# State space layer: where the discretisation stands in the first MLP, and in what pieces the scans stand among the attention's rows

## Chip, core and metric

The kernel runs on one core of one Trainium2 chip. The metric is the device time of one execution in microseconds (us); the median of three runs is quoted. The profile is one further execution with its own time. TensorE is written PE, VectorE DVE, ScalarE ACT, GpSimd POOL, and SyncE SP.

## What is computed

Six layers run one after the other on a sequence of 512 tokens with 1024 features (batch 1, fp32). The change touches two of them: the first gated MLP (stage `ffn0`) and the layer after it (stage `ssm`), in which a diagonal state space model and a latent attention read the same normed input and are joined by one output product.

```python
    dt = jnp.exp(log_dt.astype(f32))[:, None]
    mag = jnp.exp(lr * dt)
    ab_re = mag * jnp.cos(li * dt)
    ab_im = mag * jnp.sin(li * dt)
...
    _, _, x_re, x_im = lax.associative_scan(combine, (aa_re, aa_im, bu_re, bu_im), axis=1)
    y = (jnp.einsum('bsgp,ghp->bsgh', x_re, c_re.astype(f32))
         - jnp.einsum('bsgp,ghp->bsgh', x_im, c_im.astype(f32))
         + d_skip.astype(f32)[None, None] * ug)
    y = y.reshape(b, s, SSM_CHANNELS).astype(u.dtype)
    z = jax.nn.gelu(y)
    return z * jax.nn.sigmoid(z @ w_glu + b_glu)
...
        sc = jnp.einsum('bqhd,bkhd->bhqk', qb, k, preferred_element_type=f32) * scale
        p = jax.nn.softmax(jnp.where(chunk_causal_mask(i, s), sc, -jnp.inf), axis=-1)
        return jnp.einsum('bhqk,bkhd->bqhd', p.astype(v.dtype), v)
...
def swiglu(h, w_gate, w_up, w_down):
    return (jax.nn.silu(h @ w_gate) * (h @ w_up)) @ w_down
```

Here `lr` and `li` are `a_re` and `a_im`; the attention has 6 heads and 4 blocks of 128 queries. The discretisation (`dt`, `mag`, the cosines and sines, `f`) depends on parameters alone, not on the layer's input.

## The kernel before

All engines run the same six stages, and each engine's program is written by walking one list of steps, `STEPS[stage]`. A step such as `("s1", i)` makes each engine issue its own instructions for that name, if it has any, so the list fixes the order of every engine's queue. Engines wait for each other through semaphores alone. `merge(a, b)` interleaves lists in proportion to their lengths: the longer one list is in steps, the more evenly it lies in the other, and where a step falls depends on the lengths of both.

**Products.** A weight tile is 128x128. It is split into a high and a low part, and `("w", g, k)` issues three matmuls of 512 columns on PE (lines 570 to 572). Weights come in slots of eight tiles: SP loads, ACT rounds the high part (line 624), POOL subtracts to get the low part (line 2586), PE waits for the slot. There are three slots for the split weights, and ACT rounds two slots ahead.

**Stage ffn0.** 22 gates in three thirds. `fg` and `fu` are gate and up products of eight k each in two banks each; `e1`, `e2`, `e3` evict, multiply by the sigmoid, and split the result for the down products. `pend` holds those steps of one gate, and they are merged into the products of the next. `closing` is the last third's down product in eight groups of seven: three banks (4, 5, 6) in turn, which the DVE addition on line 697 frees; then comes the sum of squares for the norm (lines 610, 612), which the next stage needs. Before the change the eight steps `("ds", 0)` to `("ds", 7)`, the discretisation, are merged into all but the last 24 steps of this closing. They are chains of small DVE operations, each waiting for the one before it (lines 2133 to 2232), and on ACT `ds 0` (two Exp) and `ds 4` (four Sin with a table load ahead and one behind, lines 2388 to 2392). The last of them, `cim`, is awaited by the first softmax row of the next stage.

**Stage ssm.** The attention runs in three pairs of heads, 24 units (a head's block of 128 queries, with 512, 384, 256 or 128 keys), taken two by two. `r1` puts both units' scores into banks 2 and 3 (PE, lines 2078 to 2083); `r2` takes the row maximum (DVE, line 2290) and then the exponential (ACT, line 2454); `r3` is reciprocal and diagonal (DVE); `r4` transposes and scales the weights (PE, line 2092, copied out by ACT, line 2462); `v1`, `v2` are the values' product. The next `r1` waits until ACT has read both banks, that is for the second unit's exponential, and that waits for its maximum in DVE's queue. Besides the rows there stand the next heads' projections and the first half of the output product (`p`), evicted by ACT (line 2494).

The scan has eight parts `i`. `s1`: two small matmuls on PE (lines 2113, 2114), then four DVE products with the angles' cosine and sine (2311 to 2314). `s2`: two additions (2320, 2322) and two scans over 512 tokens (2324, 2326). `s3`: six operations that turn the result back (2332 to 2341). `s4`: eight matmuls for two parts (2125, 2127). `z1` to `z4` are the GELU, a chain through DVE and ACT, and then the product `zg`, which waits for `z_low` (line 2369). POOL computes the angles (`an`, lines 2532 to 2542); `an 5` to `an 7` wait for line 2337 of an earlier part.

Of the kernel before, what the change touches and what calls it, by code (L numbers as in the profile page):

```python
# [243 lines left out]

def steps_ffn(*besides):

    out = []
    for third, (a, b) in enumerate(THIRDS):
        pend = []
        for f in range(a, b):  # L250
            g, u = ("fg", f), ("fu", f)
            if f == 0:
                mul = opening(g, u, ("fg", 1))
            elif f == 1:
                mul = merge(group(u, 8), pend)
            else:
                mul = merge(group(g, 8) + group(u, 8), pend)
            out += mul
            pend = [("e1", f), ("e2", f), ("e3", f)]
        out += pend  # L260
        if third < 2:
            out += groups([("d", third, d) for d in range(KT)], b - a, "de")
    last = closing(THIRDS[2][1] - THIRDS[2][0])
    return out + merge(last[:-24], besides) + last[-24:] if besides else out + last

# [16 lines left out]
def steps_ssm():  # L282
# [20 lines left out]
    for i in range(0, 8, 2):  # L303
        scan += [("s1", i), ("s2", i), ("s1", i + 1), ("s3", i), ("s2", i + 1), ("s3", i + 1)]
        scan += [("an", n) for n in {0: (5,), 2: (6,), 4: (7,)}.get(i, ())]
        scan += [("s4", i)]
        if i % 4 == 2:
# [4 lines left out]


STEPS = {"even": steps_even(), "odd": steps_odd(), "diff": steps_diff(), "ffn0": steps_ffn(*[("ds", n) for n in range(8)]),
         "ssm": steps_ssm(), "ffn1": steps_ffn()}


# [163 lines left out]
def program(nc, io):  # L481
    with ExitStack() as ctx:
# [1751 lines left out]
        def dve_ssm(e):  # L2234
            s = S["ssm"]
            pe, dve, act, pool = s.pe, s.dve, s.act, s.pool
            for step in STEPS["ssm"]:
# [65 lines left out]
                elif kind == "s1":  # L2303
# [7 lines left out]
                    e.tensor_tensor(vre, ps[6][:], cosT, MUL).then_inc(dve.sem, dve.up("s_a", i))  # L2311
                    e.tensor_tensor(vim, ps[7][:], cosT, MUL).then_inc(dve.sem, dve.up("s_b", i))
                    e.tensor_tensor(w5, ps[7][:], sinT, MUL).then_inc(dve.sem, dve.up("s_c", i))
                    e.tensor_tensor(w6, ps[6][:], sinT, MUL).then_inc(dve.sem, dve.up("s_d", i))
                elif kind == "s2":
                    i = step[1]
                    vre, vim, w5, w6 = lane_of(i)
                    mg = mag[:, i:i + 1].to_broadcast([128, T])
                    e.wait_ge(dve.sem, dve["s_c", i])
                    e.tensor_tensor(vre, vre, w5, ADD).then_inc(dve.sem, dve.up("s_re", i))  # L2320
                    e.wait_ge(dve.sem, dve["s_d", i])
                    e.tensor_tensor(vim, vim, w6, SUB).then_inc(dve.sem, dve.up("s_im", i))
                    e.wait_ge(dve.sem, dve["s_re", i])
                    e.tensor_tensor_scan(w5, mg, vre, 0.0, MUL, ADD).then_inc(dve.sem, dve.up("scan_re", i))
                    e.wait_ge(dve.sem, dve["s_im", i])
                    e.tensor_tensor_scan(w6, mg, vim, 0.0, MUL, ADD).then_inc(dve.sem, dve.up("scan_im", i))
                elif kind == "s3":
# [5 lines left out]
                    e.wait_ge(dve.sem, dve["scan_im", i])  # L2333
                    e.tensor_tensor(vim, w6, cosT, MUL).then_inc(dve.sem, dve.up("s_f", i))
                    e.wait_ge(dve.sem, dve["s_f", i])
                    e.tensor_tensor(w6, w6, sinT, MUL).then_inc(dve.sem, dve.up("s_g", i))
                    e.tensor_tensor(w5, w5, sinT, MUL).then_inc(dve.sem, dve.up("s_h", i))
                    e.wait_ge(dve.sem, dve["s_g", i])
                    e.tensor_tensor(vre, vre, w6, SUB).then_inc(dve.sem, dve.up("s_i", i))
# [40 lines left out]
        def act_discretise(e, n, dve, act):  # L2380
# [4 lines left out]
            elif n == 4:  # L2385
# [5 lines left out]
                e.activation(tabs, a6, ACT.Sin, scale=6.283185).then_inc(act.sem, act.up("tabs"))  # L2391
                e.preload_act_table_set(EXP_LN)

# [365 lines left out]
```

## Time and profile before

| what | value |
|---|---|
| median of 3 runs | 2060.03 us (2060.03 to 2063.84) |
| the profiled execution | 2062.9 us, its span 2061.1 us |
| PE busy | 1815.9 us, 88% of the span |
| DVE, ACT, POOL busy | 951.9, 740.2, 925.8 us |
| chain that ended last | PE 71%, DVE 17%, ACT 7% |
| mean granted TensorE clock | 0.934 of 2.4 GHz |

The span is the time from the first to the last instruction; what lies around it is 1.8 us. PE carries most of the chain that ends last, so a microsecond in which PE waits is in general a microsecond of the kernel.

### The profile page before, as it was taken

The page shows a single profiled execution, that of the slowest core. Times are in us where ns is not written, and L with a number is a line of the kernel's source. Part 1 is how long each engine was busy: PE and PEld are TensorE (multiplying, and loading weights), DVE is VectorE, ACT ScalarE, POOL GpSimd, SP SyncE. Part 2 cuts the span into 40 slices and gives each one's busy share as a digit, 9 for nine tenths or more (in the row PEclk, how much of TensorE's full clock was granted, in tenths as well). Part 3 has the DMA queues.
Part 4 walks back from the last instruction along what each step waited for, and adds up shares of the span by engine and source line. Part 5 has one row for each costly group of instructions (what it writes and reads, how often), then busy time and mean ns, then how long its engine had stood idle before and what let it go on. Part 6 is the DMA issues. An engine that isn't in the chain of part 4 may idle for free.

```text
span 2061.1 us, 20065 instructions
## 1 busy us (share of the span) xinstructions
PE 1815.9 (88%) x7492; PEld 1363.4 (66%) x7492; DVE 951.9 (46%) x1451; ACT 740.2 (36%) x1207; POOL 925.8 (45%) x1100
## 2 busy tenths in 40 slices
PE   5999889888878898878999999988777889999996
PEld 4776456666756576455788888755454568888885
DVE  1033333677562599754430323564755554123244
ACT  4253454445344422364332322342232342322232
POOL 3433113464753354113565656468222246565563
PEclk9999999998988899988999999998778899999998
DMA  4211102212111222012233323211000122333231
GB/s 167 92 62 52 41 21 73 70 62 72 50 33 34 69 80 74 21 31 72 73 95 99 102 93 102 82 62 51 11 11 21 31 64 90 103 92 102 93 94 70
DMA packets 39553, 139.90 MB, mean 68 GB/s; under 512 B 4512, under 2 KB 4640, under 8 KB 39328
## 3 DMA queue, kind: packets, MB, share of 16 engines
q1 hardware_dynamic: 39456, 138.61, 21.1%
q8 instruction: 60, 0.98, 0.2%
q14 instruction: 37, 0.30, 0.0%
HBM read 136.50 MB, written 2.10 MB: 67 GB/s over the span
## 4 chain that ended last, share of the span: by engine, by line
PE 71%; DVE 17%; ACT 7%; issue 2%; POOL 1%; DMA 0%; SPq 0%; DVEq 0%; ACTq 0%; POOLq 0%
PE ps L570 18%; PE ps L571 17%; PE ps L572 17%; DVE ps L1689 3%; PE ps L599 2%; PE ps L583 1%; PE ps L2101 1%; PE ps L585 1%; PE ps L584 1%; PE ps L818 1%; PE ps L820 1%; POOL wl L2586 1%; PE ps L2078 1%; ACT wh L624 1%; PE ps L811 1%
## 5 line engine op out<-in xcount | busy, mean ns | idle before, releaser
L2586 POOL TENSOR_TENSOR wl<-raw,wh 128x256 fp32r<-128x256 f32 x988 | 801.7, 843 | 998.7 <-ACT wh L624 990.8
L570 PE MATMUL ps<-hh,wh 128*128 128x512 f32 x1204 | 518.5, 431 | 70.2 <-DVE hl L687 45.8
L571 PE MATMUL ps<-hl,wh 128*128 128x512 f32 x1204 | 479.5, 398 | 0.0
L572 PE MATMUL ps<-hh,wl 128*128 128x512 f32 x1204 | 478.9, 398 | 0.0
L624 ACT ACTIVATE wh<-raw 128x1024 fp32r<-128x1024 f32 x247 | 261.1, 1058 | 554.8 <-PE ps L572 507.5
L570 PEld LDWEIGHTS ps<-hh,wh 128*128 128x128 f32 x1204 | 233.2, 194 | 149.1 <-DVE hl L687 51.8
L570 PE MATMUL ps<-mh,wh 128*128 128x512 f32 x632 | 267.6, 423 | 46.1 <-DVE ml L1324 6.5
L571 PEld LDWEIGHTS ps<-hl,wh 128*128 128x128 f32 x1204 | 232.7, 193 | 61.4 <-issue 17.7
L572 PEld LDWEIGHTS ps<-hh,wl 128*128 128x128 f32 x1204 | 232.1, 193 | 50.8
L571 PE MATMUL ps<-ml,wh 128*128 128x512 f32 x632 | 254.2, 402 | 0.0
L572 PE MATMUL ps<-mh,wl 128*128 128x512 f32 x632 | 253.9, 402 | 0.0
L570 PEld LDWEIGHTS ps<-mh,wh 128*128 128x128 f32 x632 | 123.2, 195 | 95.8 <-issue 12.2
L572 PEld LDWEIGHTS ps<-mh,wl 128*128 128x128 f32 x632 | 123.3, 195 | 27.3
L571 PEld LDWEIGHTS ps<-ml,wh 128*128 128x128 f32 x632 | 124.3, 197 | 23.7 <-issue 2.0
L1899 DVE TENSOR_TENSOR ml<-arena,mh 128x512 fp32r<-128x512 f32 x44 | 34.7, 789 | 119.5 <-ACT mh L1930 119.5
L1888 DVE TENSOR_TENSOR arena<-ps,nrm 128x512 f32<-128x512 f32 x44 | 30.4, 691 | 127.7 <-PE ps L572 127.7
L1689 DVE SCALAR_TENSOR_TENSOR ps<-arena,vec,ps 128x512 f32<-128x512 f32 x116 | 87.4, 753 | 2.9
L1886 DVE TENSOR_TENSOR arena<-ps,nrm 128x512 f32<-128x512 f32 x44 | 29.9, 680 | 100.0 <-PE ps L572 100.0
L919 DVE SCALAR_TENSOR_TENSOR arena<-ps,nrm 128x128 f32<-128x128 f32 (+3 forms) x32 | 15.6, 488 | 109.5 <-ACT nrm L1005 109.5
L687 DVE SCALAR_TENSOR_TENSOR hl<-x,vec,hh 128x512 fp32r<-128x512 f32 x48 | 40.3, 839 | 53.1 <-ACT hh L639 53.1
L583 PE MATMUL ps<-wh,hh 128*128 128x512 f32 x128 | 52.1, 407 | 9.3 <-DVE arena L1160 9.2
L655 ACT ACTIVATE nrm<-arena 128x512 f32<-128x512 f32 x48 | 30.1, 627 | 77.2 <-DVE arena L697 77.1
(464 smaller groups left out, 2297.2 us busy)
## 6 DMA issues: line engine op xcount, KB each, us to landing
raw<-in_w SPq DMA_DIRECT2D x247, 512.0 KB, 3.5
x<-in_x SPq DMA_DIRECT2D x8, 256.0 KB, 6.9
out<-x SPq DMA_DIRECT2D x8, 256.0 KB, 2.0
arena<-in_rope SPq DMA_DIRECT2D x3, 512.0 KB, 4.8
arena<-in_dec SPq DMA_DIRECT2D x1, 1024.0 KB, 11.6
mats<-in_mats SPq DMA_DIRECT2D x1, 576.0 KB, 7.8
arena<-in_lw SPq DMA_DIRECT2D x1, 512.0 KB, 3.8
arena<-in_levels SPq DMA_DIRECT2D x1, 448.0 KB, 4.5
```

The lines of the kernel that those rows point to most:

```text
L570: e.matmul(ps[b][:], a, xh, start=first, stop=False)
L571: e.matmul(ps[b][:], a, xl, start=False, stop=False)
L572: e.matmul(ps[b][:], l, xh, start=False, stop=final).then_inc(pe.sem, pe.up(*step))
L583: e.matmul(ps[i][:], hh[:, k, cut(i)], a, start=(k == 0), stop=False)
L599: e.matmul(ps[7][:], M("ones"), sqr[k % 2], start=(k == 0), stop=(k == KT - 1)).then_inc(pe.sem, pe.up("sq", k))
L624: e.activation(wh[:, n % NHL, :], raw[:, n % NRAW, :], ACT.Copy).then_inc(rounded.sem, rounded.up(n))
L655: e.activation(sqr[d % 2], y[:, d, :], ACT.Square).then_inc(act.sem, act.up("oe", d))
L687: e.scalar_tensor_tensor(out=hl[:, k, :], in0=x[:, k, :], scalar=V(PRE[stage], k), in1=hh[:, k, :].bitcast(F32), op0=MUL, op1=SUB).then_in ...
L1689: e.scalar_tensor_tensor(out=yb[:, j, :] if q == 30 else conv_in[j], in0=du[:, j, q:q + T], scalar=V("dww", 4 * q + j), in1=conv_in[j], op ...
L1888: e.tensor_tensor(f_up[f % 2], ps[bank(stage, ("fu", f))][:], rb_pre, MUL).then_inc(dve.sem, dve.up("e", ("fu", f)))
L1899: e.tensor_tensor(ml[:, i, :], f_up[f % 2], mh[:, i, :].bitcast(F32), SUB).then_inc(dve.sem, dve.up("mixed", f))
L2586: e.tensor_tensor(wl[:, n % NHL, cut(i, 2)], raw[:, n % NRAW, cut(i, 2)], wh[:, n % NHL, cut(i, 2)].bitcast(F32), SUB).then_inc(split.sem, ...
```

## The change

The eight discretisation steps leave the closing of `ffn0` and stand among its gates: `ds 0` behind the opening, `ds 1`, `2`, `3` behind the gates 1, 2, 3, `ds 4` behind gate 5, `ds 5` behind gate 7 (it is then followed by the first third's down products), and `ds 6` and `7` behind the gates 8 and 9. Behind `ds 4` ACT loads the sigmoid table in place of the Exp and Ln table. In the stage `ssm` no operation is added or removed, but `s1`, `s2`, `s3` are cut into eight steps (`s1`, `s1b`, `s2`, `s2b`, `s2c`, `s3`, `s3b`, `s3c`), and the list `scan` grows from 41 steps to 81, so that `merge(mul, scan)` puts the pieces, and also `s4`, `an` and `z1` to `z4`, at other places.

```diff
-def steps_ffn(*besides):
+def steps_ffn(**besides):
...
-            pend = [("e1", f), ("e2", f), ("e3", f)]
+            pend = [("e1", f), ("e2", f), ("e3", f)] + besides.get(f"f{f}", [])
+            if f == 0:
+                out += besides.get("first", [])
...
-    last = closing(THIRDS[2][1] - THIRDS[2][0])
-    return out + merge(last[:-24], besides) + last[-24:] if besides else out + last
+    return out + closing(THIRDS[2][1] - THIRDS[2][0])
...
     for i in range(0, 8, 2):
-        scan += [("s1", i), ("s2", i), ("s1", i + 1), ("s3", i), ("s2", i + 1), ("s3", i + 1)]
+        scan += [("s1", i), ("s1b", i), ("s2", i), ("s2b", i), ("s1", i + 1), ("s1b", i + 1), ("s2c", i), ("s3", i), ("s3b", i)]
+        scan += [("s3c", i), ("s2", i + 1), ("s2b", i + 1), ("s2c", i + 1), ("s3", i + 1), ("s3b", i + 1), ("s3c", i + 1)]
         scan += [("an", n) for n in {0: (5,), 2: (6,), 4: (7,)}.get(i, ())]
         scan += [("s4", i)]
...
-STEPS = {"even": steps_even(), "odd": steps_odd(), "diff": steps_diff(), "ffn0": steps_ffn(*[("ds", n) for n in range(8)]),
+STEPS = {"even": steps_even(), "odd": steps_odd(), "diff": steps_diff(), "ffn0": steps_ffn(first=[("ds", 0)], f1=[("ds", 1)], f2=[("ds", 2)], f3=[("ds", 3)], f5=[("ds", 4)], f7=[("ds", 5)],
+                                                                         f8=[("ds", 6)], f9=[("ds", 7)]),
...
                     e.tensor_tensor(vre, ps[6][:], cosT, MUL).then_inc(dve.sem, dve.up("s_a", i))
                     e.tensor_tensor(vim, ps[7][:], cosT, MUL).then_inc(dve.sem, dve.up("s_b", i))
+                elif kind == "s1b":
...
                     e.tensor_tensor(vim, vim, w6, SUB).then_inc(dve.sem, dve.up("s_im", i))
+                elif kind == "s2b":
...
                     e.tensor_tensor_scan(w5, mg, vre, 0.0, MUL, ADD).then_inc(dve.sem, dve.up("scan_re", i))
+                elif kind == "s2c":
...
                     e.tensor_tensor(vim, w6, cosT, MUL).then_inc(dve.sem, dve.up("s_f", i))
+                elif kind == "s3b":
...
                     e.tensor_tensor(w5, w5, sinT, MUL).then_inc(dve.sem, dve.up("s_h", i))
+                elif kind == "s3c":
...
-                e.preload_act_table_set(EXP_LN)
+                e.preload_act_table_set(SIGMOID)
```

In the changed kernel the lines up to 2313 stand three lower than before, those behind them up to 21 lower.

The queue of DVE in the closing of `ffn0`, between the additions that free bank 5 (`ps5`) and bank 4 (`ps4`). Before:

```order
L697 TENSOR_TENSOR arena<-ps5,arena 128x512
L705 TENSOR_TENSOR nrm<-nrm 128x512
L697 TENSOR_TENSOR arena<-ps6,arena 128x512
L705 TENSOR_TENSOR nrm<-nrm 128x512
L2186 TENSOR_TENSOR arena<-arena 128x384
L2188 TENSOR_SCALAR arena<-arena 128x384
L2189 TENSOR_TENSOR small<-small 128x8
L2191 TENSOR_SCALAR small<-small 128x8
```

The same place now:

```order
L700 TENSOR_TENSOR arena<-ps5,arena 128x512
L708 TENSOR_TENSOR nrm<-nrm 128x512
L700 TENSOR_TENSOR arena<-ps6,arena 128x512
L708 TENSOR_TENSOR nrm<-nrm 128x512
L700 TENSOR_TENSOR arena<-ps4,arena 128x512
```

All small operations are gone from here; 19 of them stood between the last two rows (`ds 5` and `ds 6`), and others ahead of and behind this piece.

The queue of DVE where the second pair of heads meets its first scores, between the maxima of unit 8 (`ps2`) and unit 9 (`ps3`). Before:

```order
L2290 TENSOR_REDUCE small<-ps2 128x1
L2332 TENSOR_TENSOR hh_scratch_49<-hh_scratch_49 128x512
L2334 TENSOR_TENSOR hl_scratch_50<-hl_scratch_50,hh_scratch_49 128x512
L2336 TENSOR_TENSOR hl_scratch_50<-hl_scratch_50 128x512
L2337 TENSOR_TENSOR hh_scratch_49<-hh_scratch_49,hl_scratch_50 128x512
L2339 TENSOR_TENSOR hh_scratch_49<-hh_scratch_49,hl_scratch_50 128x512
L2341 TENSOR_TENSOR hl_scratch_50<-hl_scratch_50,hh_scratch_49 128x512
L2290 TENSOR_REDUCE small<-ps3 128x1
```

The same place now (the scan is printed as SCALAR_TENSOR_TENSOR):

```order
L2293 TENSOR_REDUCE small<-ps2 128x1
L2326 TENSOR_TENSOR hh_scratch_49<-hh_scratch_49 128x512
L2328 TENSOR_TENSOR hl_scratch_50<-hl_scratch_50 128x512
L2293 TENSOR_REDUCE small<-ps3 128x1
L2334 SCALAR_TENSOR_TENSOR hh_scratch_49<-small,hh_scratch_49 128x512
L2340 SCALAR_TENSOR_TENSOR hl_scratch_50<-small,hl_scratch_50 128x512
```

Six operations between the two maxima have become two, and the scans follow behind the second.

The queue of PE near the end of the stage's mixed part: the last `s4` (`ps5`) and the last two heads' values (`ps4`). Before:

```order
L2092 MATMUL ps4<-nrm 128x128 x2
L2125 MATMUL ps5<-hh_scratch_49,arena 32x512 x2
L2127 MATMUL ps5<-hl_scratch_50,arena 32x512 x2
L570 MATMUL ps1<-mh,wh 128x512
L571 MATMUL ps1<-ml,wh 128x512
L572 MATMUL ps1<-mh,wl 128x512
L2092 MATMUL ps4<-nrm,arena 128x128 x2
```

Now:

```order
L2104 MATMUL ps4<-arena 128x512
L2104 MATMUL ps4<-arena 128x384
L2104 MATMUL ps4<-arena 128x256
L2104 MATMUL ps4<-arena 128x128
L2128 MATMUL ps5<-hh_scratch_49,arena 32x512 x2
L2130 MATMUL ps5<-hl_scratch_50,arena 32x512 x2
L573 MATMUL ps0<-mh,wh 128x512
```

The last `s4` has moved from the last rows of the attention to behind both values' products; seven products of `p` remain behind it ahead of `zg`, where 11 products and both values' products stood before.

## Rows read from the trace of the kernel before

**Rows 1.** Windows: stretch, us; each engine's busy time (count); PE clock; DMA.

```profile
985.00:1307.30 322.30, 320.86 (x1407) 263.32 (x1406) 96.08 (x123) 95.42 (x120) 190.64 (x232) 1.00 0.30 93
1307.35:1353.42 46.07, 40.23 (x170) 31.26 (x169) 33.65 (x68) 17.13 (x24) 21.35 (x27) 1.00 0.24 72
2004.41:2044.07 39.66, 39.28 (x171) 31.64 (x169) 14.96 (x19) 11.68 (x15) 19.86 (x24) 1.00 0.15 48
1414.20:1633.80 219.60, 173.78 (x599) 105.99 (x598) 134.90 (x218) 56.56 (x124) 65.62 (x61) 0.77 0.06 20
```

**Rows 2.** What PE waited for, 1307 to 1356 us: total, times, longest.

```profile
PE ps L570 <- DVE arena L697: 2.8, 3, 1.5
PE ps L570 <- POOL wl L2586: 1.7, 2, 1.0
```

**Rows 3.** The same from 1414 to 1634 us.

```profile
PE ps L2078 <- ACT nrm L2454: 27.6, 6, 6.4
PE ps L570 <- DVE nrm L2281: 5.9, 2, 3.2
PE ps L570 <- ACT arena L2494: 3.8, 1, 3.8
...
PE ps L2125 <- DVE hl_scratch L2341: 2.2, 1, 2.2
```

**Rows 4.** Timeline of DVE: each MLP closing's last addition (start, duration).

```profile
1352.74 0.68 DVE L697 TENSOR_TENSOR arena<-ps,arena 128x512 f32<-128x512 f32 x1
2043.38 0.69 DVE L697 TENSOR_TENSOR arena<-ps,arena 128x512 f32<-128x512 f32 x1 [2.32 <-PE ps L572]
```

**Rows 5.** Timeline of ACT: a rounding among the gates, then around `ds 4`.

```profile
1296.73 1.06 ACT L624 ACTIVATE wh<-raw 128x1024 fp32r<-128x1024 f32 x1 [3.86 <-PE ps L572]
1328.21 1.28 ACT L2388 ACT_TABLE_LOAD   x1
1331.95 1.06 ACT L624 ACTIVATE wh<-raw 128x1024 fp32r<-128x1024 f32 x1
```

**Rows 6.** Timeline of PE: the scores of units 2 and 10.

```profile
1445.80 1.62 PE L2078 MATMUL ps<-arena 128*128 128x384 f32 x2 [3.94 <-ACT nrm L2454]
1509.29 2.26 PE L2078 MATMUL ps<-arena 128*128 128x384 f32 x3 [5.34 <-ACT nrm L2454]
```

**Rows 7.** Timeline of DVE: maxima (L2290) and scan pieces around five waits.

```profile
1502.44 0.69 DVE L2290 TENSOR_REDUCE small<-ps 128x1 f32<-128x512 f32 x1 [1.52 <-PE ps L2083]
1507.64 0.68 DVE L2290 TENSOR_REDUCE small<-ps 128x1 f32<-128x512 f32 x1
1562.19 1.22 DVE L2324 TENSOR_TENSOR_SCAN hh_scratch<-small,hh_scratch 128x512 f32<-128x512 f32 x1
1564.44 0.67 DVE L2290 TENSOR_REDUCE small<-ps 128x1 f32<-128x512 f32 x1
1587.87 1.74 DVE L2324 TENSOR_TENSOR_SCAN hh_scratch<-small,hh_scratch 128x512 f32<-128x512 f32 x1
1591.13 0.39 DVE L2290 TENSOR_REDUCE small<-ps 128x1 f32<-128x256 f32 x1
1600.05 0.69 DVE L2311 TENSOR_TENSOR hh_scratch<-ps,hh_scratch 128x512 f32<-128x512 f32 x1 [8.53 <-PE ps L2114]
1610.62 0.27 DVE L2290 TENSOR_REDUCE small<-ps 128x1 f32<-128x128 f32 x1
```

**Rows 8.** Timeline: the last GELU (DVE, ACT) and the product behind it (PE).

```profile
1620.33 0.75 DVE L2347 SCALAR_TENSOR_TENSOR arena<-arena,vec,ps 128x512 f32<-128x512 f32 x1 [3.06 <-PE ps L2127]
1623.02 0.43 DVE L2356 TENSOR_SCALAR hh_scratch<-hh_scratch 128x512 f32<-128x512 f32 x1
1626.26 0.63 ACT L2474 ACTIVATE hl_scratch<-hh_scratch 128x512 f32<-128x512 f32 x1
1633.70 1.15 DVE L2369 TENSOR_TENSOR hl<-arena,hh 128x512 fp32r<-128x512 f32 x1 [0.70 <-ACT hh L2487]
1634.90 0.50 PE L570 MATMUL ps<-hh,wh 128*128 128x512 f32 x1
```

More of the change, by code:

```diff
@@ L2312, in dve_ssm @@
                     e.tensor_tensor(vim, ps[7][:], cosT, MUL).then_inc(dve.sem, dve.up("s_b", i))
+                elif kind == "s1b":
+                    i = step[1]
+                    vre, vim, w5, w6 = lane_of(i)
+                    cosT, sinT = angle_at[i]
                     e.tensor_tensor(w5, ps[7][:], sinT, MUL).then_inc(dve.sem, dve.up("s_c", i))
@@ L2317, in dve_ssm @@
                     vre, vim, w5, w6 = lane_of(i)
-                    mg = mag[:, i:i + 1].to_broadcast([128, T])
                     e.wait_ge(dve.sem, dve["s_c", i])
@@ L2322, in dve_ssm @@
                     e.tensor_tensor(vim, vim, w6, SUB).then_inc(dve.sem, dve.up("s_im", i))
+                elif kind == "s2b":
+                    i = step[1]
+                    vre, vim, w5, w6 = lane_of(i)
+                    mg = mag[:, i:i + 1].to_broadcast([128, T])
                     e.wait_ge(dve.sem, dve["s_re", i])
                     e.tensor_tensor_scan(w5, mg, vre, 0.0, MUL, ADD).then_inc(dve.sem, dve.up("scan_re", i))
+                elif kind == "s2c":
+                    i = step[1]
+                    vre, vim, w5, w6 = lane_of(i)
+                    mg = mag[:, i:i + 1].to_broadcast([128, T])
                     e.wait_ge(dve.sem, dve["s_im", i])
@@ L2334, in dve_ssm @@
                     e.tensor_tensor(vim, w6, cosT, MUL).then_inc(dve.sem, dve.up("s_f", i))
+                elif kind == "s3b":
+                    i = step[1]
+                    vre, vim, w5, w6 = lane_of(i)
+                    cosT, sinT = angle_at[i]
                     e.wait_ge(dve.sem, dve["s_f", i])
@@ L2337, in dve_ssm @@
                     e.tensor_tensor(w5, w5, sinT, MUL).then_inc(dve.sem, dve.up("s_h", i))
+                elif kind == "s3c":
+                    i = step[1]
+                    vre, vim, w5, w6 = lane_of(i)
                     e.wait_ge(dve.sem, dve["s_g", i])
```

## The prediction

> **What bounds the kernel now.** I read the windows of four stretches first. Among the gates PE is busy for 320.86 of 322.30 us at the full clock, while DVE and ACT are each busy for 30% [rows 1]: nothing is to be gained there, and there is room for work. In the closing of `ffn0` PE is busy for 40.23 of 46.07 us, in the closing of `ffn1`, which runs the same 56 products without `ds` steps, for 39.28 of 39.66 [rows 1]. In the mixed part of `ssm` PE is busy for only 173.78 of 219.60 us, and the mean granted clock is 0.77 [rows 1], so it stands at 1.2 GHz for 46% of the time, 101 us. Both losses are PE's, and PE carries the chain, so they count in full.
>
> The waits of PE give names to them. In the closing it waits for bank releases by DVE's addition and for POOL's split of weights [rows 2]. In `ssm` the largest item is six waits, 27.6 us together, of a score product for the second exponential of the pair before; then the key products wait for the rotated query (5.9), a `p` product for its eviction on ACT (3.8), and the last `s4` for the scan's output (2.2) [rows 3]. The timelines show why: DVE is busy for 134.90 of the 219.60 us [rows 1], so it is seldom short of time, but the pair's second maximum stands behind a burst of scan work.
>
> **The discretisation.** Removed from the closing of `ffn0`: all `ds` steps, 49 DVE operations, and six on ACT with two table loads. From the first down product to the end of the last addition `ffn0` takes 46.07 us, `ffn1` 39.66 [rows 1, 4]. I take the twin as the closing without them: a gain of **6.4 us**. PE's named waits there are 2.8 + 1.7 us [rows 2]; the rest is the last addition lagging behind its products, on which the norm and the next stage wait. So the bounds are 4.5 and 6.4.
>
> Added among the gates: the same operations. DVE has 226 us free there, ACT 227 (322.30 less 96.08, and less 95.42) [rows 1]. The longest piece on ACT is `ds 4`, 3.74 us from its table load to the next rounding [rows 5]. A rounding among the gates starts after ACT has waited 3.86 us for PE [rows 5] and is made two slots ahead, that is 16 products of 0.68 us (320.86 us over 1407 matmuls, three each), 10.9 us; with 1.06 us on ACT and about 4 on POOL some 5.8 us are spare, which 3.74 does not use up. If that cover were gone, it would cost 3.74 us once. `ds 0` makes DVE wait for ACT's Exp ahead of the first gate's eviction; behind it stands only the release of a bank that PE wants eight products (5.4 us) later. Cost 0. No DMA is moved, and SP's queue is unchanged; POOL's order is unchanged too.
>
> **The scan's pieces, wait by wait.** PE's work is the same; I follow DVE's queue up to each wait.
>
> Rotation of the first query. It stood behind the four `s1` products, which waited for PE; the longest wait is 3.2 [rows 3]. Now `s1`, `s1b` start earlier, and two additions stand ahead of it. I take 1.5 gained, bounds 0 and 3.2.
>
> Unit 2, wait 3.94 [rows 6]. `s1 1` stood on PE and on DVE between the scores of units 0, 1 and their maxima; now it is ahead of them. What remains is two maxima and an exponential less two products, about 1. **Gain 2.9.** But `s21`'s two additions now stand between the maxima of units 2 and 3: **loss 0.8** (two of about 0.6, partly under products).
>
> Unit 6: the same operations lie between the maxima of units 2 and 5 in both orders, so 0.
>
> Unit 10, wait 5.34 [rows 6]. The maxima of units 8 and 9 are 5.20 us apart, of which 0.6 is the maximum itself [rows 7]. Of six operations two (1.2) stay. They cannot give more than the wait; 4.6 less 1.2 is 3.4, and two of the six ran beside POOL's angles at twice their time (which now start later), so I take **4.0 gained**. Unit 12: the `s4` that used to fill PE's time there is now behind, so PE waits for its exponential: **loss 0.8**.
>
> Unit 14: ACT's three GELU operations leave the place ahead of its exponential (2.0), but the five of `z1` now stand between its two maxima on DVE (3.1, by the same chain in [rows 8]), and they wait for an `s4`. **Gain 0.4**, bounds a loss of 3.1 and a gain of 2.0. The third query's rotation gets `s14` ahead of it: **loss 1.1**.
>
> Unit 18: both scans go from between the maxima of 16 and 17, 1562.19 to 1564.44 [rows 7]. **Gain 2.25.** Unit 22: the same, from 1587.87 to 1591.13, where POOL's split slows them [rows 7]. **Gain 3.3.**
>
> The `p` eviction, wait 3.8 [rows 3], stands on ACT behind the exponential of unit 23. From the last `s1` to that maximum DVE works for 10.57 us [rows 7]; now the pieces ahead of it are `s1`, `s1b`, `s2c`, `s3`, `s3b` and small ones, 6.6 us. **Gain 3.8**, all of the wait. The last `s4` no longer waits, since both values' products precede it: **gain 2.2** [rows 3].
>
> The tail. `z1` to `z4` follow that `s4`. Unhindered they take 3.1 (1620.33 to 1623.45), three on ACT of 0.63 to 0.72 with handovers, 2.1, and five more between the engines, 4.1 [rows 8]: 9.3 us. Before, 11 products and two values' products covered it, and `zg` started as `z_low` ended (1634.85 against 1634.90) [rows 8]. Now seven products, 4.8 us, and one of `zg` cover it: 9.3 less 5.5 is **a loss of 3.8**.
>
> Sum: 1.5 + 2.9 - 0.8 + 4.0 - 0.8 + 0.4 - 1.1 + 2.25 + 3.3 + 3.8 + 2.2 - 3.8 = 13.85 us.
>
> **The clock.** The mixed part has the waits and the low clock, the gates have neither [rows 1]. If the slow time shrank with the waits (13.85 of 219.60 less 173.78, 30%), 30 us would run at full speed, and with PE busy for 79% that is 12 us; if it does not shrink, 0 [rows 1]. Several long waits stay and a new one comes at the tail, so I take a third: **4 us**.
>
> Together 6.4 + 13.85 + 4 = 24.2 us, from the profiled execution's 2062.9: 2038.7. That execution stands 2.9 us above the median of the runs shown, so on the median the forecast is **2036 us**.
>
> The Trainium skill's page "TensorE: Matmul & The Clock Gate" (section "HAM oscillation — how this bites in real kernels") says that waits between groups of matmuls bring the clock down to half again, and puts the price at half of the slow time. By that, if all 101 us of slow time went, 50 us less would be spent; the sum above goes by the two bounds from the rows.
>
> **Rivals.**
>
> *Pieces between the maxima (slower).* DVE's order now has something between the two maxima of four more pairs (units 2 and 3, 4 and 5, 12 and 13, 18 and 19) where they stood together. If the work that left the place between other maxima (4.0, 2.25, 3.3, and 3.8 ahead of the `p` eviction) only comes back ahead of the next pair's first maximum, the gain is 0, and the four new pieces cost 1.2 us each, 3.1 for `z1`, about twice that where POOL runs beside them: up to 13.4, with the tail's 3.8 some 17. Against the 6.4 of the closing that is 11 slower: 2071. It decides where DVE is not idle ahead of a pair's first maximum. For it: one scan took 1.74 in place of 1.22 us beside POOL [rows 7]. Against it: DVE is idle for 84.7 of 219.6 us [rows 1], and waited for the scores of unit 8 (1.52) [rows 7].
>
> *POOL beside the pieces.* The angles start when `s3b` ends, so they run beside what follows at once. The Trainium skill's page "SBUF — State Buffer" (section "Who interferes with whom") says that a DVE operation with two SBUF inputs and a POOL operation that reads SBUF exclude each other for a whole instruction. As a mechanism of this kernel: the scan's pieces ahead of units 12 and 14 go from 0.6 to about 1.2 each, as the scan of 1.74 did in part [rows 7]. Eight of them on the path cost 5 us, and the forecast becomes 2041.
>
> *The scan's part gives nothing.* DVE's whole work between rows is unchanged, and each wait moves to the next pair. Then only the closing counts: 2060.03 - 6.4 = 2054.
>
> *The clock gives all.* The freed waits end most slow stretches: 12 us in place of 4, 2028.
>
> *The discretisation is not free.* If `ds 4` or `ds 3` held up a slot of weights, the closing's gain would lose up to 3.74: 2040.
>
> **How the numbers follow.** Forecast (with POOL's and the discretisation's variants) 0.58, range 2030 to 2044; scan gives nothing 0.2; clock gives all 0.14; slower 0.05; something else near no change 0.03. The range from 2022 to 2054 leaves out the slower rival, the last, and what of the third lies above its centre. Faster by over 0.2% (4 us, about what a measurement of this kernel tells from no change): 0.91; within 0.2%: 0.04; slower: 0.05.
>
> **What would show it.** Right: no wait of PE among the gates; 39 to 40 us from the first down product of `ffn0`'s last third to the last addition; the wait for the second exponential down from 27.6 to about 17 us; no wait for the eviction of `p`; a new wait of some 4 us ahead of `zg`; a mean clock above 0.77 in the mixed part, and that part shorter by 15 to 20 us. Wrong: new waits for a reciprocal's diagonal, or for the first exponential of a pair; slots of weights late among the gates; an unchanged length of the mixed part.

## The result, and the profile after

The changed kernel takes **2046.26 us** (median of four, 2045.88 to 2047.01); the kernel before, on the same chip, 2061.94. The ratio is 0.9919, with a 95% interval from 0.9904 to 0.9935: faster by 15.7 us by the medians and 16.7 by the ratio. The forecast was 2036, with a range of 2022 to 2054: the sign and the range hold, and the gain is two thirds of what was forecast (24). Below, one execution of `e6_before_pool_off` that took 3605 us, where the other nine took 2049 to 2062, is left out.

First the windows of the kernel after (stretch and its length; busy time and count of PE, PEld, DVE, ACT, POOL; clock; DMA; PEld is the loading of weights into PE, beside its products): the gates, the closing of `ffn0`, what lies between, the mixed part of `ssm`, the rest.

```profile
985.00:1307.40 322.40, 320.96 (x1407) 263.41 (x1406) 118.31 (x172) 99.62 (x128) 191.10 (x232) 1.00 0.29 93
1307.42:1346.40 38.98, 38.98 (x171) 31.72 (x169) 14.33 (x19) 13.43 (x16) 21.73 (x28) 1.00 0.32 98
1346.40:1407.30 60.90, 49.65 (x175) 34.67 (x175) 29.41 (x37) 25.30 (x37) 40.95 (x42) 0.92 0.15 50
1407.30:1618.00 210.70, 170.23 (x603) 103.99 (x601) 139.29 (x218) 57.30 (x125) 70.78 (x63) 0.80 0.07 23
1618.00:2044.40 426.40, 400.52 (x1717) 323.61 (x1717) 154.04 (x193) 132.49 (x167) 227.51 (x276) 0.97 0.27 87
```

The gates took 22 us more of DVE (96.08 to 118.31) and 0.1 us more of time. The closing went from 46.07 us to 38.98, and PE is never idle in it [rows 1]. The mixed part went from 220.6 us (1414.28 to 1634.90) to 210.7. Nothing else moved: 7.1 + 9.9 us is the whole difference of the two spans, 16.7, within 0.3 us (both in the profiles).

What PE waited for in the mixed part after (total, times, longest), beside [rows 3]:

```profile
PE ps L2081 <- ACT nrm L2475: 12.9, 6, 4.2
PE ps L2081 <- ACT arena L2475: 10.4, 3, 7.1
PE ps L573 <- DVE nrm L2284: 7.2, 3, 3.2
PE ps L2095 <- ACT arena L2483: 3.4, 7, 1.0
PE ps L573 <- ACT arena L2515: 2.7, 1, 2.7
PE ps L2104 <- DVE ml L2304: 1.8, 2, 1.6
```

`L2475` writes both `nrm` and `arena`: it is the exponential, and which of the two is named depends only on the unit. The six waits of 27.6 us are now 12.9, but three others, of which the longest is 7.1 us, stand beside them (10.4 together; before there were two, of 1.5). The wait of a `p` product for an eviction (3.8) and that of the last `s4` (2.2) are gone; those of `zg` (2.7 and 0.6) and of a value (1.6, `L2304`) are new. `L2515`, for which `zg` waits, is again an eviction of `p`: the first product of `zg` takes the bank that it frees, and on ACT it now stands behind the last GELU's exponential. That is not what holds the stage up, since the second product of `zg` waits for `z_low` behind it:

```profile
1615.22 0.63 ACT L2504 ACTIVATE hl_scratch<-hl_scratch 128x512 f32<-128x512 f32 x1 [0.76 <-DVE hl_scratch L2382]
1615.76 0.58 ACT L2515 ACTIVATE arena<-ps 128x512 f32<-128x512 f32 x1
1616.48 0.47 PE L573 MATMUL ps<-hh,wh 128*128 128x512 f32 x1 [2.67 <-ACT arena L2515]
1618.02 0.56 PE L573 MATMUL ps<-hh,wh 128*128 128x512 f32 x1 [0.62 <-DVE hl L2390]
```

The timeline of PE has the three waits for the exponential as `arena` (start, duration; in brackets the wait ahead):

```profile
1448.51 2.04 PE L2081 MATMUL ps<-arena 128*128 128x256 f32 x4 [7.11 <-ACT arena L2475]
1504.29 1.10 PE L2081 MATMUL ps<-arena 128*128 128x256 f32 x4 [0.41 <-ACT arena L2475]
1563.03 1.40 PE L2081 MATMUL ps<-arena 128*128 128x256 f32 x4 [2.92 <-ACT arena L2475]
```

They are units 4, 12 and 20. In the table below are the waits of PE at each place, taken from such rows, for the kernels that the text comes to. "No late angles" (`e5_after_pool_off`), "respaced" (`e8_before_order`), "respaced + discretisation" (`e11_blocks_best`) and "one move" (`e9_before_one_move`) are experiments that are told below; u2 is unit 2. The waits of transposes and values for ACT's copies are left out; they are 4.7 us before, 4.9 after and 8.0 respaced.

| wait at, us | before | after | after, no late angles | before, one move | before, respaced | respaced + discretisation |
|---|---|---|---|---|---|---|
| first rotation | 3.2 | 3.2 | 3.1 | 0 | 0 | 0 |
| other rotations | 2.6 | 4.0 | 4.0 | 2.6 | 1.1 | 1.1 |
| u2 | 3.9 | 0.8 | 0.8 | 4.0 | 1.6 | 1.6 |
| u4 | 1.1 | 7.1 | 2.3 | 3.6 | 4.1 | 2.9 |
| u6 | 5.0 | 1.4 | 1.4 | 3.5 | 0 | 0.3 |
| u10 | 5.3 | 2.0 | 1.9 | 5.3 | 0.8 | 0.8 |
| u12 | 0 | 0.4 | 1.0 | 0 | 0.7 | 0.7 |
| u14 | 3.4 | 4.2 | 2.5 | 3.4 | 2.0 | 2.0 |
| u18 | 3.5 | 1.3 | 1.3 | 3.5 | 3.5 | 3.5 |
| u20 | 0.4 | 2.9 | 2.1 | 0.4 | 0 | 0 |
| u22 | 6.4 | 3.2 | 3.2 | 6.4 | 0 | 0 |
| eviction of `p` | 3.8 | 0 | 0 | 3.7 | 0 | 0 |
| `s4` | 2.2 | 0 | 0 | 2.2 | 10.6 | 9.2 |
| values, `zg` | 0 | 5.1 | 4.5 | 0 | 0.4 | 0.4 |
| mixed part, us | 220.6 | 210.7 | 197.5 | 213.6 | 191.4 | 190.0 |

The mixed part of each is the profiled span, less the 426.3 us that all of them take from `zg` on, less the start of the stretch. Lines of a kernel with an edit are shifted by a few: `L2079`, `L2081` and `L2094` are the score product of `L2078` before.

### The profile page after: what moved, and what is told of

Same layout as the page of the kernel before. It is cut to its first block, busy times and chain, and to the rows that moved or that the text cites. A ratio compares the mean times of both kernels' runs of the same rounds, so it can differ in the third digit from the quotient of the medians.

```text
span 2044.4 us, 20065 instructions
## 1 busy us (share of the span) xinstructions
PE 1811.9 (89%) x7492; PEld 1362.9 (67%) x7492; DVE 958.1 (47%) x1451; ACT 740.1 (36%) x1207; POOL 928.4 (45%) x1100
## 4 chain that ended last, share of the span: by engine, by line
PE 72%; DVE 16%; ACT 7%; issue 2%; POOL 2%; DMA 0%; SPq 0%; DVEq 0%; ACTq 0%; POOLq 0%
PE ps L573 18%; PE ps L574 18%; PE ps L575 18%; DVE ps L1692 3%; PE ps L602 2%; PE ps L586 1%; PE ps L588 1%; PE ps L587 1%; PE ps L821 1%; PE ps L823 1%; PE ps L2081 1%; PE ps L2104 1%; POOL wl L2607 1%; PE ps L814 1%; DVE arena L676 1%
## 5 line engine op out<-in xcount | busy, mean ns | idle before, releaser
L602 PE MATMUL ps<-nrm,mats 128*128 128x512 f32 x96 | 52.7, 632 | 0.0
```

Of the source, the lines that this page charges most:

```text
L602: e.matmul(ps[7][:], M("ones"), sqr[k % 2], start=(k == 0), stop=(k == KT - 1)).then_inc(pe.sem, pe.up("sq", k))
```

## The experiments

Two questions: do the two halves of the change give what they were forecast to give, each by itself, and where do the waits at units 4 and 20 come from, which no term of the forecast had?

### The two halves apart

`e1_ds_only` is the kernel before with the discretisation steps among the gates:

```diff
...
-    return out + merge(last[:-24], besides) + last[-24:] if besides else out + last
+    return out + closing(THIRDS[2][1] - THIRDS[2][0])
...
-STEPS = {... "ffn0": steps_ffn(*[("ds", n) for n in range(8)]),
+STEPS = {... "ffn0": steps_ffn(first=[("ds", 0)], f1=[("ds", 1)], f2=[("ds", 2)], f3=[("ds", 3)], f5=[("ds", 4)], ...
...
```

> The first half of the change alone: the eight discretisation steps stand among the gates, the scan keeps its blocks. If the two halves are independent (mine): the closing falls from 46.07 us to about 39, the mixed part stays at 220 to 221 us, and the kernel takes 2054 to 2055 us (7 us under before). Rival, that shorter work ahead of the mixed part changes the clock granted in it: the mixed part moves by more than 1.5 us either way, and the time is off 2054.5 by as much. Rival, that the last exponentials' table load is paid in the open: 1.3 us more than mine.

`e2_scan_only` is the changed kernel with that edit taken back.

> The second half alone: single operations of the scan as steps, the discretisation in the closing as before. If the halves are independent (mine): closing 46.1 us, mixed part 210.5 to 211.5 us, the kernel 2051 to 2053 us (10 us under before), with the waits of units 4 and 20 at about 7 and 3 us as in the changed kernel. Rival, that units 4's wait comes of the discretisation's absence (VectorE reaching the mixed part in another state): the wait of unit 4 stays at 1 us and the time is 2046 to 2048.

Measured: `e1_ds_only` 2057.28 us, ratio 0.9964 (0.9949 to 0.9979), 7.4 us; `e2_scan_only` 2054.98, ratio 0.9951 (0.9933 to 0.9968), 10.1 us. Both times lie about 2 us above what I expected, and so does the kernel before beside them (2064.52 us, where it was 2061.94), so the ratios are what to read. The windows of the mixed part, `e1_ds_only` first, then `e2_scan_only`:

```profile
1408.56:1629.20 220.64, 174.81 (x602) 106.75 (x600) 135.90 (x218) 56.98 (x125) 66.63 (x62) 0.78 0.06 20
```

```profile
1414.42:1625.10 210.68, 170.07 (x603) 103.88 (x601) 139.33 (x218) 57.35 (x125) 70.89 (x62) 0.80 0.07 23
```

They are the mixed parts of before and of after to 0.1 us, with the same clock and with busy times within 0.2 us. The halves are independent and add up (0.9964 times 0.9951 is 0.9915, measured 0.9919). Unit 4's wait is in the scan's half (7.13 us in `e2_scan_only`, 1.06 in `e1_ds_only`), so the rivals of both expectations fall.

### GpSimd's late angles

Between the maximum of unit 1 and that of unit 5 DVE never rests in the changed kernel, and `an 5` runs on POOL beside it. `e3_no_late_angles` takes `an 5` to `an 7` out of the changed kernel's list, `e4_before_no_late_angles` out of the list of before. Both leave out the angles of parts 5 to 7:

```diff
...
-        scan += [("an", n) for n in {0: (5,), 2: (6,), 4: (7,)}.get(i, ())]
+        scan += []
...
-                    e.wait_ge(pool.sem, pool["sin", i])
+                    e.wait_ge(pool.sem, pool["sin", min(i, 4)])
...
```

> The changed kernel without GpSimd's angle steps of parts 5 to 7; it leaves out those angles, so that parts 5 to 7 of the scan are turned by angles that belong to other parts; VectorE's and TensorE's work is the same. If the missed 6 us at unit 4 and 2.5 us at unit 20 come of GpSimd slowing VectorE's operations beside it (mine): the additions and products between the maxima of units 1 and 5 go from 1.1 to 1.75 us back to about 0.7, unit 4's wait from 7.1 to under 2.5 us, unit 20's from 2.9 to about 0.5, and the kernel takes 2036 to 2041 us. If they come of the order alone (pieces of the scan between two maxima, rival): those waits stay above 5.5 and 2.5 us and the time is 2045 to 2047.

> The kernel before without the same three angle steps (leaves out the angles of parts 5 to 7 in the same way). If GpSimd's slowing costs the kernel before as much as the changed one (the blocks stand beside it as well as the pieces do): about 2053 to 2056 us, as much below before as the other is below the changed kernel. If it costs only where the pieces stand between maxima (mine, in part): 2057 to 2060 us, so that the change's gain without GpSimd's work beside it is over 18 us, where it was 16 with it. Under 1 us off before would mean that the blocks were never slowed on the path.

Measured: `e3_no_late_angles` 2032.28 us, ratio 0.9844 (0.9826 to 0.9861); `e4_before_no_late_angles` 2028.95, ratio 0.9823 (0.9801 to 0.9846). The first came out below what I expected. The second was below the lowest that any theory had by 24 us: without these three steps the kernel before is as fast as the changed one, or faster. But the two runs change two things. `merge(mul, scan)` spaces the scan's steps evenly among the products, and with three entries fewer in `scan` all others stand at slightly different places. So the next four runs fill in the square: POOL's work kept or not, the old spacing or the new.

In `e5` and `e6` POOL skips its steps (the wait for them is changed as above) and every order stays:

```diff
...
-            if step[0] == "an":
+            if step[0] == "an" and step[1] < 5:
...
```

In `e7` and `e8` POOL does them, and they are put in behind the merge:

```diff
-        scan += [("an", n) for n in {0: (5,), 2: (6,), 4: (7,)}.get(i, ())]
...
-    out += merge(mul, scan)
+    late = {("s4", 0): 5, ("s4", 2): 6, ("s4", 4): 7}
+    for step in merge(mul, scan):
+        out += ([("an", late[step])] if step in late else []) + [step]
```

> The run without late angles also moved steps, because the scan's list became three entries shorter and the merge spaces it anew. Here every engine keeps the order of the changed kernel, and GpSimd alone does nothing for the angles of parts 5 to 7 (left out: those angles; parts 5 to 7 turn by others). If GpSimd's work beside VectorE is what cost (theory A): 2030 to 2036 us, unit 4's wait under 2.5 us. If the new spacing gave the 14 us (theory B): 2042 to 2046 us.

> The same in the kernel before: its own order on every engine, GpSimd without the angles of parts 5 to 7 (left out as above). Theory A: 2030 to 2038 us, 25 to 32 under before. Theory B: 2050 to 2060 us, since most of the 33 us came of the new spacing.

> The other cell: the changed kernel with all its work, but the three angle steps are not counted when the scan's list is merged with the products; they are put directly ahead of the last step of parts 0, 2 and 4 afterwards. Nothing is left out. Theory A: 2042 to 2050 us, as the changed kernel. Theory B: 2031 to 2036 us. If it lies between, both take part.

> The same spacing in the kernel before, with all its work. Theory A: 2056 to 2066 us. Theory B: 2030 to 2040 us, that is below the changed kernel: then the kernel before lost to where its blocks fell, not to their being blocks.

Medians, with the ratio to before and its interval:

| | old spacing | respaced |
|---|---|---|
| blocks (before), all angles | 2061.94, 1 | **2035.99**, 0.9860 (0.9842 to 0.9877) |
| blocks, no late angles | 2053.69, 0.9956 (0.9940 to 0.9972) | 2028.95, 0.9823 (0.9801 to 0.9846) |
| pieces (the change), all angles | 2046.26, 0.9919 (0.9904 to 0.9935) | 2040.12, 0.9888 (0.9869 to 0.9907) |
| pieces, no late angles | 2035.47, 0.9862 (0.9847 to 0.9877) | 2032.28, 0.9844 (0.9826 to 0.9861) |

The pieces have the discretisation's 7 us in them, the blocks do not. A difference of two of these ratios is known to 4 or 5 us only. The profiled mixed parts are sharper: in the two pairs of runs with equal order and equal work (before and `e1_ds_only`, after and `e2_scan_only`) they agree to 0.1 us, while the stages ahead, which no edit here touches, took 3 to 6 us more in the profiles of `e4`, `e6` and `e8` than in that of before. The windows of `e6_before_pool_off`, `e8_before_order`, `e5_after_pool_off` and `e7_after_order`:

```profile
1419.06:1629.50 210.44, 168.20 (x602) 102.70 (x600) 129.64 (x218) 56.99 (x125) 44.39 (x44) 0.80 0.06 20
1417.22:1608.60 191.38, 158.39 (x608) 96.05 (x607) 136.62 (x218) 56.30 (x126) 68.18 (x62) 0.86 0.07 23
```

```profile
1409.26:1606.80 197.54, 164.73 (x604) 101.40 (x603) 127.02 (x218) 57.22 (x125) 45.86 (x44) 0.83 0.08 24
1408.34:1612.80 204.46, 164.77 (x602) 99.59 (x600) 136.00 (x218) 56.84 (x125) 66.95 (x62) 0.83 0.07 24
```

The fourth cells, `e4_before_no_late_angles` and `e3_no_late_angles`, have 183.2 and 196.3 us. Three readings.

POOL's angles cost the changed kernel 12 us at the old spacing and 9 at the new, and the kernel before 9 and 8 (differences of the ratios; 13.2, 8.2, 10.2 and 8.2 in the mixed parts). Theory A (POOL's work is what cost) was right for the changed kernel and three times too large for the kernel before. The change itself therefore made POOL's work dearer by some 3 us only. Where it acts can be seen in the timelines, of DVE and POOL in the kernel after, and then of DVE alone in `e5_after_pool_off`, at the same place:

```profile
1438.79 1.05 POOL L2553 TENSOR_TENSOR mh_scratch<-arena 128x512 f32<-128x512 f32 x1 [7.04 <-DVE small L2298]
1438.82 1.10 DVE L2300 TENSOR_SCALAR nrm<-mats,small 128x128 f32<-128x128 f32 x1
1439.79 1.05 POOL L2556 TENSOR_TENSOR nrm<-arena 128x512 f32<-128x512 f32 x1
1439.84 1.55 DVE L2360 TENSOR_TENSOR hh_scratch<-hh_scratch,hl_scratch 128x512 f32<-128x512 f32 x1
1440.92 1.59 POOL L2558 TENSOR_TENSOR mh_scratch<-mh_scratch,nrm 128x512 f32<-128x512 f32 x1
1441.31 1.74 DVE L2362 TENSOR_TENSOR hl_scratch<-hl_scratch,hh_scratch 128x512 f32<-128x512 f32 x1
```

```profile
1438.99 0.29 DVE L2300 TENSOR_SCALAR nrm<-mats,small 128x128 f32<-128x128 f32 x1
1439.19 0.69 DVE L2360 TENSOR_TENSOR hh_scratch<-hh_scratch,hl_scratch 128x512 f32<-128x512 f32 x1
1439.80 0.69 DVE L2362 TENSOR_TENSOR hl_scratch<-hl_scratch,hh_scratch 128x512 f32<-128x512 f32 x1
```

The same two operations take 1.55 and 1.74 us beside POOL and 0.69 without it, and 1.74 is the 0.69 of the one and the 1.05 of the other, one after the other. The Trainium skill's page "SBUF — State Buffer" (section "Who interferes with whom") has the two take turns by whole instructions where the DVE operation has two SBUF inputs; the trace agrees. Unit 4's wait falls from 7.11 to 2.30 us and unit 14's from 4.23 to 2.48; unit 20's only from 2.92 to 2.13. The waits of PE together shrink by less than 8 us; the mixed part shrinks by 13.2, and PE's busy time in it from 170.2 to 164.7 us, as its clock goes from 0.80 to 0.83.

The spacing alone gives the kernel before 29 us (ratio 0.9860, and 29.2 in the mixed parts): theory B (the spacing gives it), and in blocks. It gives the pieces 6. And in the new spacing the version in pieces is the slower one: the pieces stand at 0.9888 with the discretisation in them, which by itself is 0.9964, so at 0.9924 without it, where the blocks stand at 0.9860, 13 us less (204.5 and 191.4 us in the mixed parts).

So what does the new spacing have? PE's waits in the respaced kernel before, at units 10, 14, 18, and in none at 22:

```profile
1495.50 0.88 PE L2079 MATMUL ps<-arena 128*128 128x384 f32 x2 [0.84 <-ACT nrm L2455]
1511.62 0.57 PE L2079 MATMUL ps<-arena 128*128 128x128 f32 x3 [2.03 <-ACT nrm L2455]
1550.52 1.97 PE L2079 MATMUL ps<-arena 128*128 128x384 f32 x3 [3.50 <-ACT nrm L2455]
1572.69 0.60 PE L2079 MATMUL ps<-arena 128*128 128x128 f32 x4
```

And the maxima of DVE ahead of units 10, 18 (two rows) and 22 (a row with x2 is both maxima of a pair, back to back):

```profile
1493.17 1.29 DVE L2291 TENSOR_REDUCE small<-ps 128x1 f32<-128x512 f32 x2 [1.52 <-PE ps L2084]
1544.83 0.69 DVE L2291 TENSOR_REDUCE small<-ps 128x1 f32<-128x512 f32 x1 [1.22 <-PE ps L2084]
1548.88 0.67 DVE L2291 TENSOR_REDUCE small<-ps 128x1 f32<-128x512 f32 x1
1570.67 0.73 DVE L2291 TENSOR_REDUCE small<-ps 128x1 f32<-128x256 f32 x2
```

In the kernel before, blocks of the scan stand between the maxima of units 8 and 9 (`s3 3`), 16 and 17 (`s2 5`), 20 and 21 (`s2 6`), 5.20, 4.06 and 5.86 us apart [rows 7]. After the respacing only the one between 16 and 17 is left, 4.05 us apart, and it alone still costs PE its 3.50 us (3.48 before); the other two pairs are together, and 5.34 and 6.37 us of PE's waits have become 0.84 and nothing. The change made what stands between these maxima shorter. The respacing takes it away. No run moves these blocks and nothing else: the two waits are 10.9 us of what the respaced kernel gains, and it also gains at other places, loses 8.4 us at `s4` and 3.0 at unit 4, and has 16.4 us less of busy PE at a clock of 0.86.

### One move at the first rotation

The respaced kernel before differs in one more place: `s1 0` stands behind the addition that ends the first query's rotation, not ahead of it, and PE does not wait there. `e9_before_one_move` makes this one move in the kernel before, `e10_after_one_move` in the changed kernel (where `s1 0`, `s1b 0` and `s2 0` go behind).

```diff
-    out += merge(mul, scan)
+    mixed = merge(mul, scan)
+    held = [step for step in mixed if step in [("s1", 0)]]
+    mixed = [step for step in mixed if step not in held]
+    at = mixed.index(("qb", 0)) + 1
+    out += mixed[:at] + held + mixed[at:]
```

> One move in the kernel before: the first products of part 0 of the scan, which stand ahead of the addition that ends the first query's rotation, go directly behind it. In the respaced kernel the rotation's wait of 3.3 us was gone and the second unit's scores began 11 us sooner after the start of the mixed part. Theory C (an early wait costs more than itself, since the clock granted to the matmuls behind it falls with it): 2052 to 2056 us, 8 to 11 under before, half the clock between 12 and 31 us gone. Theory D (a wait is worth its length): 2059 to 2061 us. If the respaced kernel owed its 27 us to the other moves: within 2 us of before.

> The same move in the changed kernel: the first products, second products and additions of part 0 go behind the rotation's addition. Theory C: 2035 to 2039 us, 8 to 11 under the changed kernel; the mixed part 200 to 203 us instead of 210.7. Theory D: 2043 us. No gain (2045 to 2047) if the 3.2 us only moves to the second unit's wait.

Measured: `e9_before_one_move` 2057.28 us, ratio 0.9972 (0.9956 to 0.9989); `e10_after_one_move` 2044.99, ratio 0.9908 (0.9880 to 0.9935), which cannot be told from the changed kernel's 0.9919. Windows of `e9_before_one_move` from the start of the mixed part to the scores of unit 2, and of the kernel before:

```profile
1415.39:1438.40 23.01, 18.22 (x76) 10.86 (x74) 19.34 (x22) 7.64 (x14) 21.30 (x18) 0.93 0.15 46
```

```profile
1414.28:1445.80 31.52, 23.55 (x75) 14.40 (x74) 20.05 (x22) 7.72 (x14) 22.50 (x20) 0.76 0.16 50
1426.24:1445.80 19.56, 15.62 (x47) 9.68 (x48) 13.18 (x13) 4.27 (x9) 12.09 (x10) 0.67 0.09 28
```

Unit 2 comes 8.5 us sooner, for a wait of 3.2: the same matmuls (75 and 76 rows) are busy for 18.22 us, not 23.55, because PE behind the wait stood at 1.2 GHz for two thirds of 19.56 us (clock 0.67). But then unit 4 waits 3.59 us for its exponential, where it waited 1.08, since DVE has the same work in less time, and the mixed part is shorter by 7.0 us in the end (5.8 by the ratio, with an interval from 2.3 to 9.1). The 7.0 lies between theory C, that an early wait costs more than itself (8 to 11), and D, that it is worth its length (3); the interval of the ratio alone would tell neither from the other. In the changed kernel the rotation's wait goes too, but another comes at its place: the small matmuls of part 1 (`L2120`) want the banks that `s1b 0` frees, which now runs later. PE's wait before unit 2 and the window up to it:

```profile
PE ps L2120 <- DVE hl_scratch L2325: 1.8, 1, 1.8
```

```profile
1411.43:1439.30 27.87, 24.57 (x75) 14.44 (x73) 18.96 (x22) 7.67 (x14) 22.44 (x20) 0.76 0.19 57
```

The mixed part is shorter by 2.1 us only, as the last of the three expectations has it: the wait moved, if not to unit 2.

### A version below both

`e11_blocks_best` is the respaced kernel before plus the discretisation among the gates. `e12_pieces_best` is the respaced changed kernel with every piece between two maxima of a pair put behind the second, and none ahead of a rotation's end.

```diff
...
+    for n in range(0, 24, 2):
+        a, b = mixed.index(("r2", n)), mixed.index(("r2", n + 1))
+        held = [s for s in mixed[a:b] if s[0][0] in "sz" or s[0] == "an"]
+        mixed = mixed[:a] + [s for s in mixed[a:b] if s not in held] + [("r2", n + 1)] + held + mixed[b + 1:]
...
```

> A version meant to beat both: the discretisation among the gates as in the change, the scan in blocks as before, respaced as in the run of 2036 us. The discretisation was worth 7.1 us by itself, so 2028 to 2031 us if the two add up. Over 2034 would mean that they share something.

> The respaced changed kernel (2040 us) with its pieces moved away from the places that cost: no piece between the two maxima of a pair of units, and none of part 0, 2 and 4 ahead of the addition that ends a rotation. Theory C: 2024 to 2031 us, since the three rotations' waits (3.1, 1.2, 2.4 us), unit 4's and unit 20's (3.6, 3.0 us) shrink and the clock rises with them. Theory D: 2031 to 2035 us. Above 2036 the places weren't what cost.

Measured: `e11_blocks_best` **2026.48 us**, ratio 0.9820 (0.9795 to 0.9845), below the changed kernel by 1.0%; `e12_pieces_best` 2032.80, ratio 0.9854 (0.9833 to 0.9875). The window of the mixed part in `e11_blocks_best`, and then in `e12_pieces_best`:

```profile
1406.95:1596.90 189.95, 159.17 (x608) 97.60 (x607) 136.62 (x218) 56.15 (x126) 68.20 (x62) 0.85 0.07 23
```

```profile
1407.78:1605.30 197.52, 162.55 (x602) 98.59 (x600) 138.82 (x218) 56.22 (x125) 67.79 (x62) 0.84 0.08 24
```

The first came out 1.5 us under its expectation. The second lies in theory D's range (2031 to 2035), 1.8 us above theory C's: 7 us less than `e7_after_order`, by the ratios and in the mixed part (204.5 to 197.5). Its waits (total, times, longest) say where the gain came from, and where not:

```profile
PE ps L2094 <- ACT arena L2488: 10.5, 3, 4.8
PE ps L2094 <- ACT nrm L2488: 8.1, 5, 4.5
...
PE ps L586 <- ACT arena L2528: 3.1, 2, 2.7
PE ps L2129 <- DVE hl_scratch L2334: 2.5, 3, 1.8
PE ps L2108 <- DVE nrm L2313: 2.1, 1, 2.1
PE ps L2117 <- DVE ml L2317: 1.8, 1, 1.8
```

`L2313` is a diagonal of reciprocals, `L2317` a value's rounding. The gain is mostly at the rotations: their three waits (3.15, 1.10 and 2.61 in `e7_after_order`) are gone and 2.5 us for banks (`L2129`) stand in their place. The score products gained only 0.8 (19.5 to 18.6): with nothing between maxima, units 4 (4.76), 12 (2.10), 14 (4.48) and 20 (3.65) still wait, and 4, 12 and 20 wait longer than in `e7_after_order` (3.63, 0.47, 2.97), since what was put behind the second maximum stands ahead of the next pair's first. And the tail's wait for `zg` (2.7) and those of the last heads' values (2.1, 1.8) are there, which no kernel in blocks has at over 0.3 us.

## Why the prediction was right, and where it was off

**The closing.** Forecast 6.4 us, bounds 4.5 and 6.4; measured 7.1 in the profile, just outside the bounds, and 7.4 (4.3 by the interval's near end) in `e1_ds_only`. The twin in `ffn1` was the right model, and a little worse than the real thing: it has 0.4 us in which PE is idle, and this one none.

**The gates.** Forecast 0. They took 0.1 us more, with no new wait of PE. Right; the covers held.

**The scan.** Forecast 13.85 us of waits and 4 of the clock. Measured 9.9 together: waits shrank by 5.4 (45.8 us of the mixed part without busy PE, now 40.5), busy time by 4.6. The prediction wanted the mixed part shorter by 15 to 20 us. Its waits' sum was two and a half times too large, which is the step that was mis-sized. The clock's term came out right partly by luck. Its rule was that the slow time shrinks with the waits, 12 us for 13.85, and the forecast took a third of that. The same rule with the 5.4 us of waits that were gained (5.4 of 45.8, of 101 us of slow time, with PE busy for 79%, half of it saved) gives 4.7, and 4.6 was measured: the rule held in full, and the third made up for the waits that did not go. Of the waits' terms:

- Right within 0.6 us: unit 2 (3.1 measured, 2.9 forecast), unit 10 (3.4 against 4.0), unit 12 (-0.4 against -0.8), unit 18 (2.2 against 2.25), unit 22 (3.2 against 3.3), the `p` eviction (3.8), the last `s4` (2.2), the third rotation (-1.4 against -1.1), the tail (-3.3 against -3.8, at `zg`, two waits of 2.67 and 0.62; `z_low`, which the forecast named, ends the second).
- Mis-sized: **"Unit 6: the same operations lie between the maxima of units 2 and 5 in both orders, so 0", and unit 3's maxima at 0.8.** Together units 4 and 6 lost 2.4 us (6.1 to 8.5). The operations were the same; the time at which they ran was not. In the new order `an 5` slows six of them, by 4.8 us together, and the run without it gives back 4.8 of unit 4's 7.1. Without POOL's steps units 4 and 6 together wait 3.3 us before (`e6_before_pool_off`) and 3.7 after (`e5_after_pool_off`), 0.4 lost, within the forecast's 0.8: so what was mis-sized here is POOL. This is the rival *POOL beside the pieces*, which had 5 us and the wrong place (units 12 and 14; there it was 1.2 in all).
- Missing: **unit 20**, -2.5. A piece (`s3b 5`) stands between the maxima of 18 and 19, which are 2.59 us apart. The forecast named this pair among the four new ones in its slower rival and left it out of its sum. POOL's steps are only 0.8 of its wait.
- Missing: **the value at `L2304`**, -1.6. ACT had the product's high part ready at 1602.18 us, and DVE started on the rounding at 1603.80, behind four operations of part 7.
- Wrong: **the first rotation**, +1.5 forecast, 0.1 measured. The four `s1` products start earlier, but two additions stand behind them and ahead of the rotation, and beside `an 3` they last 1.53 us each. `e10_after_one_move` puts them behind, and then PE waits for a bank at the same place instead.
- Unit 14 lost 0.8 where 0.4 was to be gained; within its bounds.

**The rivals.** *The clock gives all* needed 12 us of clock, and the change gave 4.6. But where more waits go, the clock gives as much: `e11_blocks_best` has a mixed part of 190.0 us, with PE busy for 159.2, against 220.6 and 174.7. Half of these 30.6 us, 15.5, are busy time of the same products. *The scan's part gives nothing* fell by `e2_scan_only`. *Pieces between the maxima* was right in mechanism at units 4 and 20, where pieces hold the maxima of a pair 3.14 and 2.59 us apart, and it cost less than the gain. The forecast did not see that the blocks moved elsewhere whole give more than cut in place. How much of that comes of clearing the place between two maxima is not shown: in `e12_pieces_best` that alone gave next to nothing.

**What stays open.** Why pieces are slower than blocks in the two best kernels: 197.5 us against 190.0 for the mixed part. The traces say where: the pieces wait 6.8 us longer at the score products (18.6 against 11.8), 6.7 at values and `zg` (7.1 against 0.4) and 1.4 at rotations and their banks, but 9.2 less at `s4` and 2 less for ACT's copies; the other 3.4 us are busy time of PE. Whether the cutting or the places cause this was not tested. In the best kernel the largest wait is one of 6.9 us for the last `s4`; nothing was tried against it. The spacing that was found is the one that three entries fewer happened to give; no other one was tried.

## What to carry to other kernels

Where a helper spaces two lists evenly, adding or cutting entries moves everything else too: a gain read off such a change may be the spacing's, and a run that holds the order and drops the work (or the reverse) is what tells them apart. A pair of short operations for which another engine waits is best kept together where their engine has room behind them: at units 10 and 22 of the respaced kernel nearly the whole wait went. Where it has none, what is put behind the pair only stands ahead of the next one, as in `e12_pieces_best`. And before an engine's work is made to start earlier, look at what it will then run beside.

## What was not expected of the hardware

One wait of 3.2 us at the first rotation made the next 19.6 us of PE run at a granted clock of 0.67 and so cost 8.5 us by the next row of scores. In `e10_after_one_move` a wait of 1.8 us close behind that place still left the stretch up to unit 2 at a clock of 0.76 and 27.87 us, where `e9_before_one_move`, with no such wait, has 0.93 and 23.01. The Trainium skill's page "TensorE: Matmul & The Clock Gate" (section "HAM oscillation — how this bites in real kernels") has waits between groups of matmuls cost more than themselves; the traces here agree, with 8.5 for 3.2 in one place. Not all of it was kept: of those 8.5 us the later waits took back 1.5.

A DVE addition of 128x512 numbers with both inputs in SBUF took 0.69 us alone and up to 1.75 beside POOL, and a product of 128x128 by a column up to 1.24 for 0.29. Three bursts of six POOL operations, 8 us each, so cost the changed kernel 12 us in all by the ratios. In the profiles it is 13.2, of which 5.5 are in PE's busy time, with the clock at 0.80 in place of 0.83.

Over the whole mixed part, waits and clock went together: from before to `e11_blocks_best` PE's time without products fell by 15.0 us and its time busy with the same products by 15.5, from before to after by 5.4 and 4.6.
